# A two-layer hybrid trunk on one core: the second MLP's W2 with activations stationary, and TensorE's MLP loops written out

## The chip, the core and the metric

The kernel runs on one core of a Trainium2 chip. Its time is the device time of one execution in microseconds (us), and lower is better. The engines are TensorE (PE, with its weight loads listed apart as PEld), VectorE (DVE), ScalarE (ACT), GpSimd (POOL) and SyncE (SP), which issues most transfers here.

## The reference, cut to what matters

The input is 256 frames of 2048 values. 16 meta tokens are put ahead of them, which makes 272 tokens; two layers follow, and the meta tokens are dropped at the end. Layer 0 has a state-space mixer, layer 1 windowed attention; behind each mixer stands a dense MLP. Everything is float32.

```python
def squared_relu_mlp(h, w1, w2):          # w1: 2048 x 8192, w2: 8192 x 2048
    a = jax.nn.relu(h @ w1)
    return (a * a) @ w2

for i in range(DEPTH):                    # DEPTH = 2
    hn = rms_norm(h, norm_mix_gain[i])
    ...
    h = h + mix.astype(h.dtype)
    h = h + squared_relu_mlp(rms_norm(h, norm_mlp_gain[i]), mlp_w1[i], mlp_w2[i])
return h[:, N_META:]
```

## The kernel before, in words

**Layout.** The residual `h` stands transposed in SBUF, as 16 tiles of 128 model columns on the partitions by 272 tokens. Every dense product is cut the same way: the weight is the stationary operand, 128 x 128 of it at a time, and the tokens stream past it, 272 in layer 0 and 256 in layer 1's second half, where the meta tokens are no longer needed. The result is again model columns on partitions, so it can be added to `h` as it is.

**Precision.** Each fp32 product is made of three products in the type fp32r: high part by high part, high by low, low by high. ScalarE makes the high part of a weight (`split_hi`, L236, `whi<-raw`), VectorE the low part (`split_lo`, L241, `wlo<-raw,whi`). The activations are split likewise, into `hg_hi` and `hg_lo` for W1 and into `a_hi` and `a_lo` for W2 (the last by `low`, L375).

**Weight stream.** Weights come in halves of 256 rows by 512 columns, 512 KB each, into a ring of RING = 4 slots. SP issues a half (L228) when `lo_split` says that the half four before it has been split; ScalarE may overwrite `whi` when TensorE has used the half four before (`half_used`). The counters run through the whole kernel.

**The MLPs.** An MLP has 8 chunks of 1024 hidden columns. A chunk has six groups: two of W1, each 8 halves for 512 hidden columns, then four of W2, each 4 halves for 512 model columns. `mm_half` multiplies one half: 4 column blocks by 2 row blocks by 3 products, so 24 matmuls, all at L257. That is 384 matmuls for a chunk's W1 and 384 for its W2. Groups take turns in two sets of four PSUM banks. After a W1 group VectorE takes relu and scale out of PSUM (L388), ScalarE squares and rounds (L420, L422), VectorE makes `a_lo` (L375). After a W2 group VectorE adds the four banks to `h` (L397). TensorE may start a group when the group two before it has been taken out (`group_out`), and the third half of a chunk's first W2 group waits for `a_ready` of the second W1 group.

**Loops.** On every engine chunk 0 is written out, chunks 1 to 6 are a hardware loop (`Fori(1, 7)`; TensorE's are L646 in layer 0 and L785 in layer 1), and chunk 7 is written out again. In the loop the counts to wait for are worked out in registers (L250, L267, L361).

**The end.** TensorE transposes the finished `h` back, 32 transposes of 128 x 128 (L794), ScalarE and VectorE copy the banks to `ob` (L1028, L1532), and SP stores eight blocks of 256 KB (L495).

Of the kernel before, what the change touches and what calls it, by code (L numbers as in the profile page):

```python
# [40 lines left out]
RING = 4  # L41
# [47 lines left out]
def trunk(nc, x, meta, g_mix, g_mlp, w_in, log_dt, a_re, a_im, b_re, b_im, c_re, c_im, d_skip,  # L89
# [24 lines left out]
    with ctx:  # L114
# [95 lines left out]
        hg3_lo = at(AR + 34816, "hg3_lo", [128, KT, L], F32R)  # L210
        gained = [(hg_hi, hg_lo)] * 3 + [(hg3_hi, hg3_lo)]

        ob = at(AR + 17408, "ob", [128, 8, 512])
        bias_dram = nc.dram_tensor("bias_by_distance", (NH, NREL), F32, kind="Internal").ap()

        s_raw = [sem(f"raw_landed{k}") for k in range(RING)]
# [122 lines left out]

        def mlp_pe(pe, H, G, layer, c, i, cols):
            def c_val(base, per):
                return base + per * c if i is None else base + per * i
            h0, g0 = (H + 32 * c, G + 6 * c) if i is None else (H, G)
            atok = slice(0, cols.stop - cols.start)
            k = 1 + 2 * layer
            for g in range(2):
                def ready(j):
                    if i is None and c == 0 and g == 0 and j % 2 == 0:  # L350
                        pe.wait_ge(sem("hg_ready"), 4 * k + j // 2 + 1)
                    if i is None and c == 0 and g == 0 and j == 6:
                        pe.wait_ge(sem("group_out"), g0)
                        norm_pe(pe, k, STAT_BANK[k], cols)
                if i is None and c == 0 and g == 1:
                    pe.wait_ge(sem("var_ready"), k + 1)
                mm_group(pe, h0 + 8 * g, i, g0 + g, i, *gained[k], 8, cols, ready)
            for g in range(4):
                def ready(j):
                    if g == 0 and j % 2 == 0:  # L360
                        pe.wait_ge(sem("a_ready"), c_val(16 * layer + j // 2 + 1, 2))  # L361
                mm_group(pe, h0 + 16 + 4 * g, i, g0 + 2 + g, i, a_hi, a_lo, 4, atok, ready)

        def mlp_dve(dve, H, G, layer, c, i, cols, last_chunk):
            h0, g0 = (H + 32 * c, G + 6 * c) if i is None else (H, G)
            n = cols.stop - cols.start
            k = 1 + 2 * layer

            def a_count(m):
                return 16 * layer + 2 * c + m if i is None else 16 * layer + m + 2 * i  # L370

            def low(g):

                dve.wait_ge(sem("a_hi_ready"), a_count(g + 1))
                nc.vector.tensor_tensor(a_lo[:, 4 * g:4 * g + 4, 0:n], asq[:, :, 0:n],  # L375
                                        a_hi[:, 4 * g:4 * g + 4, 0:n], ALU.subtract).then_inc(sem("a_ready"), 1)

            for j in range(32):
                ends = {7: 0, 15: 1, 19: 2, 23: 3, 27: 4, 31: 5}.get(j)
                if ends is not None:  # L380
                    if ends == 0 and i is None and c == 0:
                        norm_rstd_dve(dve, k, cols)
                    dve.wait_ge(sem("half_used"), half(h0 + j + 1, i))
                    src = acc[:, 4 * ((g0 + ends) % 2):4 * ((g0 + ends) % 2) + 4, 0:n]
                    if ends < 2:
                        if layer or ends or i is not None or c:
                            dve.wait_ge(sem("a_sq_ready"), a_count(ends))
                        nc.vector.scalar_tensor_tensor(  # L388
                            out=rbuf[:, :, 0:n], in0=src, scalar=0.0,
                            in1=view(rstd[:, cols], [[0, 4], [1, n]]),  # L390
                            op0=ALU.max, op1=ALU.mult).then_inc(sem("group_out"), 1)
                    else:
                        g = ends - 2

                        dve.wait_ge(sem("group_out"), g0 + ends - 5 if i is None else g0 + ends - 5 + 6 * i)
                        dst = h[:, 4 * g:4 * g + 4, cols]
                        nc.vector.tensor_tensor(dst, dst, src, ALU.add).then_inc(sem("group_out"), 1)  # L397
                if h0 + j + RING < H_END:
                    split_lo(dve, h0 + j + RING, i)
                if ends in (0, 1):  # L400
                    low(ends)
                if last_chunk and ends is not None and ends >= 2 and layer == 0:
                    norm_dve(dve, 2, ends - 2, ALLT)
# [51 lines left out]
        @block.sync  # L455
        def _(sp):
            for tb in range(2):
                sp.dma_start(xs[:, tb, :], x[0, 128 * tb:128 * tb + 128, :]).then_inc(sem("x_landed"), 16)
            sp.dma_start(ms[:, :], meta).then_inc(sem("x_landed"), 16)


            sp.wait_ge(sem("vec_landed"), 16 * 10)

            def stream(h0, w, n_groups, halves, col0=0):
                for g in range(n_groups):
                    for j in range(halves):
                        src = w[256 * j:256 * j + 256, col0 + 512 * g:col0 + 512 * g + 512]
                        load_half(sp, h0 + halves * g + j, None, src.rearrange("(t p) n -> p t n", p=128))

            def stream_mlp(H, layer):  # L470
                with sp.Fori(0, 8) as c:
                    for g in range(2):
                        for j in range(8):
                            src = w1[layer, 256 * j:256 * j + 256, bass.ds(c * 1024 + 512 * g, 512)]
                            load_half(sp, H + 8 * g + j, c, src.rearrange("(t p) n -> p t n", p=128))
                    for g in range(4):
                        for j in range(4):
                            src = w2[layer, bass.ds(c * 1024 + 256 * j, 256), 512 * g:512 * g + 512]
                            load_half(sp, H + 16 + 4 * g + j, c, src.rearrange("(t p) n -> p t n", p=128))

            stream(H_IN, w_in[0], 2, 8)
            stream(H_GLU, w_glu[0], 2, 4)
            stream(H_OUT, w_out[0], 4, 4)
            stream_mlp(H_MLP0, 0)
            stream(H_QKV, w_qkv[0], 1, 8, D)
            stream(H_QKV + 8, w_qkv[0], 4, 8)
            for k, (g, j) in enumerate(WO_ORDER):
                src = w_o[0, 256 * j:256 * j + 256, 512 * g:512 * g + 512]
                load_half(sp, H_WO + k, None, src.rearrange("(t p) n -> p t n", p=128))
            stream_mlp(H_MLP1, 1)  # L490
            for g in range(4):
                for tb in range(2):

                    sp.wait_ge(sem("ob_act" if tb == 0 else "ob_dve"), g + 1)
                    sp.dma_start(out[0, 128 * tb:128 * tb + 128, 512 * g:512 * g + 512],  # L495
                                 ob[:, 2 * g + tb, :]).then_inc(sem("out_landed"), 16)
            sp.wait_ge(sem("out_landed"), 8 * 16)

        @block.tensor
        def _(pe):  # L500
# [141 lines left out]
                mm_group(pe, H_OUT + 4 * g, None, G_OUT + g, None, a_hi, a_lo, 4, ALLT, ready)  # L642


            mlp_pe(pe, H_MLP0, G_MLP0, 0, 0, None, ALLT)
            with pe.Fori(1, 7) as c:  # L646
                mlp_pe(pe, H_MLP0, G_MLP0, 0, None, c, ALLT)
            mlp_pe(pe, H_MLP0, G_MLP0, 0, 7, None, ALLT)


            def kv_stats():
# [129 lines left out]
                    attend(3, k)  # L781


            mlp_pe(pe, H_MLP1, G_MLP1, 1, 0, None, REAL)
            with pe.Fori(1, 7) as c:  # L785
                mlp_pe(pe, H_MLP1, G_MLP1, 1, None, c, REAL)
            mlp_pe(pe, H_MLP1, G_MLP1, 1, 7, None, REAL)

            for g in range(4):
                if g % 2 == 0:  # L790
                    pe.wait_ge(sem("group_out"), G_MLP1 + 47 + g // 2)
                for tb in range(2):
                    for t in range(4):
                        m = tr(acc[:, (2 * g + tb + 4) % 8, 128 * t:128 * t + 128],  # L794
                               h[:, 4 * g + t, NMETA + 128 * tb:NMETA + 128 * tb + 128], ident)
                    m.then_inc(sem("out_tr"), 1)

        @block.scalar
        def _(act):
# [223 lines left out]
            with act.Fori(1, 7) as c:  # L1023
                mlp_act(act, H_MLP1, G_MLP1, 1, None, c, REAL, False)
            mlp_act(act, H_MLP1, G_MLP1, 1, 7, None, REAL, True)
            for g in range(4):
                act.wait_ge(sem("out_tr"), 2 * g + 1)
                nc.scalar.activation(ob[:, 2 * g, :], acc[:, (2 * g + 4) % 8, :], ACT.Copy).then_inc(sem("ob_act"), 1)  # L1028

        @block.gpsimd  # L1030
        def _(pool):
# [81 lines left out]
        def _(dve):  # L1113
# [413 lines left out]
            with dve.Fori(1, 7) as c:  # L1527
                mlp_dve(dve, H_MLP1, G_MLP1, 1, None, c, REAL, False)
            mlp_dve(dve, H_MLP1, G_MLP1, 1, 7, None, REAL, True)
            for g in range(4):  # L1530
                dve.wait_ge(sem("out_tr"), 2 * g + 2)
                v.tensor_copy(ob[:, 2 * g + 1, :], acc[:, (2 * g + 5) % 8, :]).then_inc(sem("ob_dve"), 1)  # L1532


_INS = ["x", "meta_tokens", "norm_mix_gain", "norm_mlp_gain", "s5_w_in", "s5_log_dt", "s5_a_re", "s5_a_im",
# [19 lines left out]
```

## Time and profile before

| | before |
|---|---|
| three runs, median (lowest to highest) | 2160.84 us (2160.17 to 2161.29) |
| profiled execution, span from the first to the last instruction | 2160.0 us |
| mean granted TensorE clock | 0.971 |
| TensorE busy | 2019.7 us (94%), 16332 matmuls |
| VectorE, ScalarE busy | 1244.9 us (58%), 885.8 us (41%) |
| moved by DMA | 338.66 MB, mean 157 GB/s |
| layer 0's MLP, first to last matmul | 318.2 to 1138.2 us |
| layer 1's MLP, first to last matmul | 1423.1 to 2150.7 us |

The profiled execution has no time listed apart from its span; the span is 0.84 us below the median of the three runs. A line of the profile has the form "line engine operation output<-input (partitions x elements, type) xcount | busy us, mean ns of one | idle before it, and what ended most of it". L257 is line 257 of the kernel. A matmul's own duration includes filling and draining, and neighbours overlap; what one matmul costs in a stream is therefore the stretch divided by their number.

### The profile page before, as it was taken

The numbers are of one execution on the slowest core, as the hardware profiler recorded it, in microseconds if no ns is written. First come the engines' busy times: TensorE is split into PE (matmuls) and PEld (weight loads), VectorE is DVE, ScalarE is ACT, GpSimd is POOL, SyncE is SP. The second block draws the span as 40 slices with busy tenths as digits, with TensorE's granted clock in tenths as the row PEclk, the third lists the DMA queues.
The fourth block names the chain that finished last, engine by engine and source line by source line (L and its number), as shares of the span: only waits on it lengthen the run. The fifth ranks groups of instructions, "written<-read, shape, count | busy, mean of one in ns | idle before, by whom it ended". The sixth has DMA issues, their size and how long they took to land.

```text
span 2160.0 us, 39380 instructions
## 1 busy us (share of the span) xinstructions
PE 2019.7 (94%) x16332; PEld 1987.4 (92%) x16332; DVE 1244.9 (58%) x1268; ACT 885.8 (41%) x1047; POOL 155.9 (7%) x91
## 2 busy tenths in 40 slices
PE   6575797999999999999999999999999999999998
PEld 5475797999999999999999888999999999999998
DVE  6989773544545454545476666665555555555554
ACT  4251353343424343434355445554434444344443
POOL 2837300000000000000000011000000000000000
PEclk9797898999999999999999999999999999999999
DMA  6211157555555555555554423556565655656564
GB/s 183 61 43 30 57 177 169 175 174 159 176 152 175 153 175 157 176 153 175 176 170 148 142 89 113 171 167 198 187 187 185 181 189 185 186 185 184 185 185 137
DMA packets 188846, 338.66 MB, mean 157 GB/s; under 512 B 23112, under 2 KB 27416, under 8 KB 188376
## 3 DMA queue, kind: packets, MB, share of 16 engines
q1 hardware_dynamic: 171200, 331.52, 49.4%
q10 hardware_dynamic: 17384, 4.77, 1.4%
q8 instruction: 113, 1.85, 0.3%
q0 software_dynamic: 128, 0.34, 0.1%
q14 instruction: 21, 0.17, 0.0%
HBM read 334.11 MB, written 2.14 MB: 156 GB/s over the span
## 4 chain that ended last, share of the span: by engine, by line
PE 85%; DVE 11%; issue 2%; ACT 1%; ACTq 1%; DMA 0%; SPq 0%; DVEq 0%
PE acc L257 80%; DVE wlo L241 2%; DVE z L1311 1%; ACTq L927 1%; PE acc L717 1%; DVE tb L1328 1%; PE acc L721 1%; DVE hg_lo L289 1%; PE acc L690 0%; DMA ms<-in_meta_tokens 0%; DVE rot L1302 0%; DVE z L1305 0%; PE acc L588 0%; DVE rot L1308 0%; PE acc L704 0%
## 5 line engine op out<-in xcount | busy, mean ns | idle before, releaser
L241 DVE TENSOR_TENSOR wlo<-raw,whi 128x1024 fp32r<-128x1024 f32 x624 | 767.8, 1235 | 712.9 <-ACT whi L236 712.7
L236 ACT ACTIVATE whi<-raw 128x1024 fp32r<-128x1024 f32 x624 | 658.8, 1058 | 1086.4 <-PE acc L257 1066.7
L257 PE MATMUL acc<-hg_hi,whi 128*128 128x256 f32 (+1 forms) x2496 | 722.7, 290 | 54.4 <-DVE wlo L241 38.7
L257 PE MATMUL acc<-hg_hi,wlo 128*128 128x256 f32 (+1 forms) x2496 | 718.7, 288 | 11.1 <-issue 11.1
L257 PE MATMUL acc<-hg_lo,whi 128*128 128x256 f32 (+1 forms) x2496 | 716.2, 287 | 0.0
L257 PE MATMUL acc<-a_hi,whi 128*128 128x272 f32 (+1 forms) x2176 | 619.0, 284 | 1.5 <-DVE a_lo L1374 1.5
L257 PE MATMUL acc<-a_hi,wlo 128*128 128x272 f32 (+1 forms) x2176 | 617.9, 284 | 0.0
L257 PE MATMUL acc<-a_lo,whi 128*128 128x272 f32 (+1 forms) x2176 | 616.4, 283 | 0.0
L257 PEld LDWEIGHTS acc<-hg_hi,whi 128*128 128x128 f32 x2496 | 479.3, 192 | 72.4 <-issue 42.4
L257 PEld LDWEIGHTS acc<-hg_lo,whi 128*128 128x128 f32 x2496 | 477.4, 191 | 0.1
L257 PEld LDWEIGHTS acc<-hg_hi,wlo 128*128 128x128 f32 x2496 | 477.3, 191 | 0.0
L257 PEld LDWEIGHTS acc<-a_hi,whi 128*128 128x128 f32 x2176 | 409.3, 188 | 1.7 <-DVE a_lo L1374 1.7
L257 PEld LDWEIGHTS acc<-a_lo,whi 128*128 128x128 f32 x2176 | 409.5, 188 | 0.0
L257 PEld LDWEIGHTS acc<-a_hi,wlo 128*128 128x128 f32 x2176 | 408.6, 188 | 0.0
L397 DVE TENSOR_TENSOR h<-h,acc 128x1088 f32<-128x1088 f32 (+1 forms) x64 | 80.3, 1254 | 50.4 <-PE acc L257 50.4
L588 PE MATMUL acc<-um,wb 128*128 128x136 f32 x256 | 43.9, 343 | 34.5 <-DVE z L1305 32.6
L588 PEld LDWEIGHTS acc<-um,wb 128*128 128x128 f32 x256 | 42.5, 247 | 36.1 <-ACT um L863 28.9
L257 PE MATMUL acc<-o_hi,whi 128*128 128x256 f32 x256 | 72.5, 283 | 0.0
L257 PE MATMUL acc<-o_lo,whi 128*128 128x256 f32 x256 | 71.8, 280 | 0.0
L257 PE MATMUL acc<-o_hi,wlo 128*128 128x256 f32 x256 | 71.8, 280 | 0.0
L1099 POOL DMA_DIRECT2D kk<-kk x4 | 2.2, 562 | 930.4 <-DVE kk L1504 930.4
L375 DVE TENSOR_TENSOR a_lo<-asq,a_hi 128x1088 fp32r<-128x1088 f32 (+1 forms) x32 | 40.3, 1259 | 37.5 <-ACT a_hi L422 37.5
(235 smaller groups left out, 1283.9 us busy)
## 6 DMA issues: line engine op xcount, KB each, us to landing
raw<-in_mlp_w SPq DMA_DIRECT2D x512, 512.0 KB, 3.8
raw<-in_attn_w_qkv SPq DMA_DIRECT2D x40, 512.0 KB, 3.7
raw<-in_attn_w_o SPq DMA_DIRECT2D x32, 512.0 KB, 4.0
raw<-in_s_w_in SPq DMA_DIRECT2D x16, 512.0 KB, 4.1
raw<-in_s_w_out SPq DMA_DIRECT2D x16, 512.0 KB, 4.8
raw<-in_s_w_glu SPq DMA_DIRECT2D x8, 512.0 KB, 3.8
xs<-in_x SPq DMA_DIRECT2D x2, 1024.0 KB, 7.5
bias_w<-bias_by_distance ACTq DMA_DIRECT2D x2, 1024.0 KB, 13.7
```

Of the source, the lines that this page charges most:

```text
L236: nc.scalar.activation(whi[:, k, :, :], raw[:, k, :, :], ACT.Copy).then_inc(sem("hi_split"), 1)
L241: nc.vector.tensor_tensor(wlo[:, k, :, :], raw[:, k, :, :], whi[:, k, :, :], ALU.subtract).then_inc(sem("lo_split"), 1)
L257: m = nc.tensor.matmul(o, w[:, k, t, 128 * n:128 * n + 128], xx[:, kt + t, cols], start=first and t == 0 and j == 0 and not (packed and n ...
L289: last = nc.vector.scalar_tensor_tensor(out=gained[k][1][:, t, cols], in0=h[:, t, cols], scalar=vecs[:, V_GAIN + 16 * k + t:V_GAIN + 16 * ...
L375: nc.vector.tensor_tensor(a_lo[:, 4 * g:4 * g + 4, 0:n], asq[:, :, 0:n], a_hi[:, 4 * g:4 * g + 4, 0:n], ALU.subtract).then_inc(sem("a_read ...
L397: nc.vector.tensor_tensor(dst, dst, src, ALU.add).then_inc(sem("group_out"), 1)
L588: m = nc.tensor.matmul(acc[:, a, CHUNKS * part:CHUNKS * (part + 1)], wb[:, i, 1 - r, part, :], um[i % 2][:, a, r::2], start=part == 0 and ...
L717: nc.tensor.matmul(o, vw[:, 2 * pr + cp, n, :], ptw[:, par::2, CHUNK * cp:CHUNK * cp + CHUNK], start=cp == 0, stop=False, skip_group_check ...
L721: m = nc.tensor.matmul(acc[rows, 7, 128 * t:128 * t + 128], vm[:, n, 2 * t + par, :], ptm[:, :], start=False, stop=True, skip_group_check= ...
L927: act.dma_start(bias_m[64 * par:64 * par + 64, pr, :, :], bass.AP(bd.tensor, first, [[1, 64], [NREL, NH], [1, NMETA]])).then_inc(sem("bias ...
L1311: op = v.tensor_tensor_scan(out=zz[:, a, part, :], data0=view(prm[:, MAGT, 4 * i + a:4 * i + a + 1], [[0, CHUNKS]]), data1=rot[:, a, part, ...
L1328: stt(out=tb[:, :], in0=tb[:, :], scalar=1.0, in1=yb[:, i % 2, :], op0=ALU.add, op1=ALU.mult).then_inc(sem("t_made"), 1)
```

## The change

It does three things. TensorE's two MLPs are written out, 8 chunks each, with constants in their waits; the other engines keep their loops. In layer 1's MLP, W2 is multiplied the other way round (`mlp1_pe`): 128 columns of `a_hi` or `a_lo`, which are 128 tokens, are stationary, and a row block of the weight half streams by with all its 512 columns, so that the result has tokens on partitions and fills one bank for each of the two token blocks. The residual of these tokens is put into the banks at chunk 0, by 32 fp32 matmuls of `h` with the identity (8 ahead of each of the four groups); VectorE copies the two banks of chunk 0 to `out_rows`, and adds those of chunks 1 to 7 to it. At the end the transposes, the copies and `ob` are gone, and SP stores four blocks of 512 KB straight from `out_rows`.

```diff
+        out_rows = at(HG, "out_rows", [128, 2, D])
...
+        def mlp1_pe(pe, c):
...
+            for g in range(4):
+                bank = 4 * ((g0 + 2 + g) % 2)
+                pe.wait_ge(sem("group_out"), g0 + 1 + g)
+                if c == 0:
+                    for tb in range(2):
+                        for t in range(4):
+                            nc.tensor.matmul(acc[:, bank + tb, 128 * t:128 * t + 128],
+                                             h[:, 4 * g + t, NMETA + 128 * tb:NMETA + 128 * tb + 128], ident,
+                                             start=t == 0, stop=False, skip_group_check=True)
+                for j in range(4):
+                    if g == 0 and j % 2 == 0:
+                        pe.wait_ge(sem("a_ready"), 16 + 2 * c + j // 2 + 1)
+                    pe.wait_ge(sem("lo_split"), h0 + 16 + 4 * g + j + 1)
+                    k = (h0 + 16 + 4 * g + j) % RING
+                    for t in range(2):
+                        for tb in range(2):
+                            rows = slice(128 * tb, 128 * tb + 128)
+                            for n, (xx, w) in enumerate(((a_hi, whi), (a_lo, whi), (a_hi, wlo))):
+                                m = nc.tensor.matmul(acc[:, bank + tb, :], xx[:, 2 * j + t, rows], w[:, k, t, :],
+                                                     start=c > 0 and j == 0 and t == 0 and n == 0,
+                                                     stop=j == 3 and t == 1 and n == 2, skip_group_check=True)
+                    m.then_inc(sem("half_used"), 1)
...
-                        dst = h[:, 4 * g:4 * g + 4, cols]
-                        nc.vector.tensor_tensor(dst, dst, src, ALU.add).then_inc(sem("group_out"), 1)
+                        if layer:
+                            src = acc[:, 4 * ((g0 + ends) % 2):4 * ((g0 + ends) % 2) + 2, :]
+                            dst = out_rows[:, :, 512 * g:512 * g + 512]
+                        else:
+                            dst = h[:, 4 * g:4 * g + 4, cols]
+                        if layer and i is None and c == 0:
+                            nc.vector.tensor_copy(dst, src).then_inc(sem("group_out"), 1)
+                        else:
+                            nc.vector.tensor_tensor(dst, dst, src, ALU.add).then_inc(sem("group_out"), 1)
...
+                sp.wait_ge(sem("group_out"), G_MLP1 + 44 + g + 1)
+                sp.dma_start(out[0].rearrange("(b p) n -> p b n", p=128)[:, :, 512 * g:512 * g + 512],
+                             out_rows[:, :, 512 * g:512 * g + 512]).then_inc(sem("out_landed"), 16)
...
-            mlp_pe(pe, H_MLP0, G_MLP0, 0, 0, None, ALLT)
-            with pe.Fori(1, 7) as c:
-                mlp_pe(pe, H_MLP0, G_MLP0, 0, None, c, ALLT)
-            mlp_pe(pe, H_MLP0, G_MLP0, 0, 7, None, ALLT)
+            for c in range(8):
+                mlp_pe(pe, H_MLP0, G_MLP0, 0, c, ALLT)
...
-            mlp_pe(pe, H_MLP1, G_MLP1, 1, 0, None, REAL)
-            with pe.Fori(1, 7) as c:
-                mlp_pe(pe, H_MLP1, G_MLP1, 1, None, c, REAL)
-            mlp_pe(pe, H_MLP1, G_MLP1, 1, 7, None, REAL)
+            for c in range(8):
+                mlp1_pe(pe, c)
```

The order of TensorE's instructions shows it at two places. The first is the end of a chunk of layer 0's MLP. Before, where the loop turns (ISA and REGISTER_ALU rows set the counts to wait for):

```order
L257 MATMUL acc<-a_hi,whi 128x272
L257 MATMUL acc<-a_lo,whi 128x272
L257 MATMUL acc<-a_hi,wlo 128x272
L646 REGISTER_ALU
L646 COMPARE_AND_BRANCH
L257 MATMUL acc<-hg_hi,whi 128x272 [waits lo_split,group_out]
L257 MATMUL acc<-hg_lo,whi 128x272
```

The same place in the changed kernel, between chunks 1 and 2:

```order
L257 MATMUL acc<-a_hi,whi 128x272
L257 MATMUL acc<-a_lo,whi 128x272
L257 MATMUL acc<-a_hi,wlo 128x272
L257 MATMUL acc<-hg_hi,whi 128x272 [waits lo_split,group_out]
L257 MATMUL acc<-hg_lo,whi 128x272
```

The branch and the register work are gone, and the matmuls of the next chunk are the next instructions in memory.

The second place is the start of W2 in chunk 0 of layer 1's MLP, in the changed kernel (L382 is the residual, `cst` the identity; L394 the product, of which a half now has 12):

```order
L257 MATMUL acc<-hg_hi,wlo 128x256
L382 MATMUL acc<-cst,h 128x128 [waits group_out]
L382 MATMUL acc<-cst,h 128x128 x7
L394 MATMUL acc<-whi,a_hi 128x512 [waits lo_split,a_ready]
L394 MATMUL acc<-whi,a_lo 128x512
L394 MATMUL acc<-wlo,a_hi 128x512
L394 MATMUL acc<-whi,a_hi 128x512
```

And the end of the program before:

```order
L257 MATMUL acc<-a_lo,whi 128x256
L257 MATMUL acc<-a_hi,wlo 128x256
L794 MATMUL acc<-cst,h 128x128 [waits group_out]
L794 MATMUL acc<-cst,h 128x128 x15
L794 MATMUL acc<-cst,h 128x128 [waits group_out]
L794 MATMUL acc<-cst,h 128x128 x15
```

In the changed kernel the last W2 matmul is the last instruction of TensorE's work: the turning of the residual has moved from the end to chunk 0.

## Rows read from the trace of the kernel before

**Rows 1.** The page: TensorE's row, and the chain that ended last.
```profile
PE 2019.7 (94%) x16332; PEld 1987.4 (92%) x16332; DVE 1244.9 (58%) x1268; ACT 885.8 (41%) x1047; POOL 155.9 (7%) x91
...
PE 85%; DVE 11%; issue 2%; ACT 1%; ACTq 1%; DMA 0%; SPq 0%; DVEq 0%
```

**Rows 2.** Windows, layer 0's MLP: stretch, us, PE busy, PEclk, DMA share, GB/s.
```profile
430.40:526.60 96.20, 96.20 (x770) 1.00 0.57 176
...
526.60:629.00 102.40, 98.13 (x770) 0.98 0.53 165
629.00:735.60 106.60, 99.31 (x770) 0.97 0.53 163
735.60:838.60 103.00, 98.74 (x769) 0.97 0.54 164
838.60:941.40 102.80, 98.89 (x769) 0.97 0.53 164
941.40:1042.00 100.60, 97.76 (x769) 0.98 0.54 164
1042.00:1138.10 96.10, 96.10 (x769) 1.00 0.56 173
```

**Rows 3.** Timeline of PE where the loop turns: start us, us, instruction [idle before].
```profile
526.51 0.28 PE L257 MATMUL acc<-a_hi,wlo 128*128 128x272 f32 x1
529.27 0.39 PE L257 MATMUL acc<-hg_hi,whi 128*128 128x272 f32 x1 [2.49 <-issue]
...
531.94 0.38 PE L257 MATMUL acc<-hg_hi,wlo 128*128 128x272 f32 x1 [1.78 <-issue]
```

**Rows 4.** Source lines L646 and L785: duration ns min/median/max, first and last start.
```profile
L646 PEldq COMPARE_BRANCH  x6: 79/4283/4519, 524.5 to 1039.8; - x6
...
L785 PEldq COMPARE_BRANCH  x6: 76/208/237, 1604.4 to 2057.9; - x6
```

**Rows 5.** DMA by queue, 430.4 to 1042 us, then 1606 to 2060 us.
```profile
q8 instruction: 51, 0.84, 0.5%
...
q1 hardware_dynamic: 43599, 84.04, 60.1%
issues: line engine op xcount, KB each, median us to landing
raw<-in_mlp_w SPq DMA_DIRECT2D x161, 512.0 KB, 3.9
```

**Rows 6.** Windows, layer 1's MLP: W2 of chunk 0, W1 and W2 of chunk 1.
```profile
1470.60:1515.69 45.09, 45.09 (x386) 1.00 0.60 188
1515.69:1561.28 45.59, 45.59 (x387) 1.00 0.59 185
1561.28:1606.39 45.11, 45.11 (x387) 1.00 0.61 188
```

**Rows 7.** Windows, `a_lo` in the eight W2 stretches of layer 1: their sum.
```profile
sum 360.90, PE 285.23 PEld 192.66 DVE 9.81; mean PE 35.65 PEld 24.08 DVE 1.23
```

**Rows 8.** Timeline, plain fp32 matmuls: L304 (4 as 8 records), L573 (32 as 64).
```profile
1440.23 1.89 PE L304 MATMUL acc<-ssq,cst 128*128 128x256 f32 x8
...
136.65 7.23 PEld L573 LDWEIGHTS acc<-cc,bp 128*128 128x128 f32 x64
```

**Rows 9.** Timeline of DVE in chunk 1 of layer 1.
```profile
1564.93 1.23 DVE L375 TENSOR_TENSOR a_lo<-asq,a_hi 128x1024 fp32r<-128x1024 f32 x1 [1.09 <-ACT a_hi L422]
```

**Rows 10.** The page: groups of L241, L236 and L397, and the weights' DMA.
```profile
L241 DVE TENSOR_TENSOR wlo<-raw,whi 128x1024 fp32r<-128x1024 f32 x624 | 767.8, 1235 | 712.9 <-ACT whi L236 712.7
L236 ACT ACTIVATE whi<-raw 128x1024 fp32r<-128x1024 f32 x624 | 658.8, 1058 | 1086.4 <-PE acc L257 1066.7
...
L397 DVE TENSOR_TENSOR h<-h,acc 128x1088 f32<-128x1088 f32 (+1 forms) x64 | 80.3, 1254 | 50.4 <-PE acc L257 50.4
...
raw<-in_mlp_w SPq DMA_DIRECT2D x512, 512.0 KB, 3.8
```

**Rows 11.** Timeline of the end, all engines, and L495's time to landing.
```profile
2150.43 0.28 PE L257 MATMUL acc<-a_hi,wlo 128*128 128x256 f32 x1
2150.45 3.51 PEld L794 LDWEIGHTS acc<-cst,h 128*128 128x128 f32 x32
...
2150.75 1.22 DVE L397 TENSOR_TENSOR h<-h,acc 128x1024 f32<-128x1024 f32 x1 [8.90 <-PE acc L257]
...
2151.81 4.62 SPq L495 DMA_DIRECT2D out<-ob  x8
...
2154.24 0.69 DVE L1532 COPY ob<-acc 128x512 f32<-128x512 f32 x1 [0.18 <-PE acc L794]
...
DMA to landing us min/median/max: 2.5/3.5/3.8
```

More of the change, by code:

```diff
@@ L211, in trunk @@
         gained = [(hg_hi, hg_lo)] * 3 + [(hg3_hi, hg3_lo)]
-        ob = at(AR + 17408, "ob", [128, 8, 512])
+        out_rows = at(HG, "out_rows", [128, 2, D])
         bias_dram = nc.dram_tensor("bias_by_distance", (NH, NREL), F32, kind="Internal").ap()
@@ L338, in trunk, with mlp_pe @@
         STAT_BANK = [7, 4 * ((G_MLP0 + 1) % 2), 4 * ((G_QKV + 1) % 2), 4 * ((G_MLP1 + 1) % 2)]
[L342 to L345, printed above, removed]
+        def mlp_pe(pe, H, G, layer, c, cols):
+            h0, g0 = H + 32 * c, G + 6 * c
             atok = slice(0, cols.stop - cols.start)
@@ L349, in ready @@
                 def ready(j):
-                    if i is None and c == 0 and g == 0 and j % 2 == 0:
+                    if c == 0 and g == 0 and j % 2 == 0:
                         pe.wait_ge(sem("hg_ready"), 4 * k + j // 2 + 1)
-                    if i is None and c == 0 and g == 0 and j == 6:
+                    if c == 0 and g == 0 and j == 6:
                         pe.wait_ge(sem("group_out"), g0)
                         norm_pe(pe, k, STAT_BANK[k], cols)
-                if i is None and c == 0 and g == 1:
+                if c == 0 and g == 1:
                     pe.wait_ge(sem("var_ready"), k + 1)
-                mm_group(pe, h0 + 8 * g, i, g0 + g, i, *gained[k], 8, cols, ready)
+                mm_group(pe, h0 + 8 * g, None, g0 + g, None, *gained[k], 8, cols, ready)
             for g in range(4):
@@ L360, in ready @@
                     if g == 0 and j % 2 == 0:
-                        pe.wait_ge(sem("a_ready"), c_val(16 * layer + j // 2 + 1, 2))
-                mm_group(pe, h0 + 16 + 4 * g, i, g0 + 2 + g, i, a_hi, a_lo, 4, atok, ready)
+                        pe.wait_ge(sem("a_ready"), 16 * layer + 2 * c + j // 2 + 1)
+                mm_group(pe, h0 + 16 + 4 * g, None, g0 + 2 + g, None, a_hi, a_lo, 4, atok, ready)
+        def mlp1_pe(pe, c):
+            h0, g0 = H_MLP1 + 32 * c, G_MLP1 + 6 * c
+            for g in range(2):
+                def ready(j):
+                    if c == 0 and g == 0 and j % 2 == 0:
+                        pe.wait_ge(sem("hg_ready"), 12 + j // 2 + 1)
+                    if c == 0 and g == 0 and j == 6:
+                        pe.wait_ge(sem("group_out"), g0)
+                        norm_pe(pe, 3, STAT_BANK[3], REAL)
+                if c == 0 and g == 1:
+                    pe.wait_ge(sem("var_ready"), 4)
+                mm_group(pe, h0 + 8 * g, None, g0 + g, None, *gained[3], 8, REAL, ready)
+            for g in range(4):
[20 more added lines that the diff above has]
+                    m.then_inc(sem("half_used"), 1)
@@ L491, in _ @@
             for g in range(4):
[L492 to L497, printed above, removed]
+                sp.wait_ge(sem("group_out"), G_MLP1 + 44 + g + 1)
+                sp.dma_start(out[0].rearrange("(b p) n -> p b n", p=128)[:, :, 512 * g:512 * g + 512],
+                             out_rows[:, :, 512 * g:512 * g + 512]).then_inc(sem("out_landed"), 16)
+            sp.wait_ge(sem("out_landed"), 4 * 16)
         @block.tensor
@@ L781, in _ @@
                     attend(3, k)
-            mlp_pe(pe, H_MLP1, G_MLP1, 1, 0, None, REAL)
-            with pe.Fori(1, 7) as c:
-                mlp_pe(pe, H_MLP1, G_MLP1, 1, None, c, REAL)
-            mlp_pe(pe, H_MLP1, G_MLP1, 1, 7, None, REAL)
[L789 to L796, printed above, removed]
+            for c in range(8):
+                mlp1_pe(pe, c)
         @block.scalar
@@ L1025, in _ @@
             mlp_act(act, H_MLP1, G_MLP1, 1, 7, None, REAL, True)
-            for g in range(4):
-                act.wait_ge(sem("out_tr"), 2 * g + 1)
-                nc.scalar.activation(ob[:, 2 * g, :], acc[:, (2 * g + 4) % 8, :], ACT.Copy).then_inc(sem("ob_act"), 1)
         @block.gpsimd
@@ L1529, in _ @@
             mlp_dve(dve, H_MLP1, G_MLP1, 1, 7, None, REAL, True)
-            for g in range(4):
-                dve.wait_ge(sem("out_tr"), 2 * g + 2)
-                v.tensor_copy(ob[:, 2 * g + 1, :], acc[:, (2 * g + 5) % 8, :]).then_inc(sem("ob_dve"), 1)
 _INS = ["x", "meta_tokens", "norm_mix_gain", "norm_mlp_gain", "s5_w_in", "s5_log_dt", "s5_a_re", "s5_a_im",
```

## The prediction

> **What bounds the kernel now.** I read the page first: TensorE is busy for 94% of the span and holds 85% of the chain that ended last [rows 1]. So what counts is how long TensorE's stream of matmuls is, and where it has holes. The view by windows gives both. In layer 0's MLP a whole chunk (768 matmuls of 272 columns) takes 96.2 us where it runs undisturbed, in chunk 1 and in chunk 7, which is 125.3 ns a matmul at a granted clock of 1.00; chunks 2 to 6 take 102.4, 106.6, 103.0, 102.8 and 100.6 us, at 0.97 or 0.98 [rows 2]. The timeline shows the holes: where the loop turns, nothing starts for 2.5 us, five matmuls run, then again nothing for 1.8 us, and both idle times end by "issue", so TensorE waited for no other engine [rows 3]. The branch that turns the loop takes 4.3 us in the median [rows 4], and the queue that brings TensorE's instructions is active all the while: 51 packets of 16 KB in 612 us, so one each 12 us [rows 5].
>
> Layer 1's MLP has the same loop and no such holes. There the branch takes 0.2 us [rows 4], the instruction queue is absent from 1606 to 2060 us [rows 5], and chunk 1's W1 and W2 take 45.59 and 45.11 us with TensorE busy throughout [rows 6]. The loop's body evidently stays at hand in layer 1, while in layer 0 it is fetched anew each turn.
>
> **Part 1, layer 0's MLP written out.** With the branch gone, chunks 2 to 6 should run like chunks 1 and 7. Chunk 7 is the right model: it is straight-line code today, fetched as it goes, and has no hole. From 526.6 to 1042.0 us are 515.4 us; 5 x 96.2 = 481.0. **Gain 34.4 us**, holes and the slower clock behind them together. The weights must keep up without those pauses: chunk 7 did at 173 GB/s and layer 1 runs at 185 to 188 [rows 2, 6], so they will. The low end, if a third of the excess is something else, is 23 us.
>
> The Trainium skill (Runtime: NRT & Kernel Launch, section Instruction fetch mechanics) says that TensorE holds 128 KiB of instructions, refilled in blocks of 16 KiB, and that a taken branch to a target outside what is held stalls for a fetch. Layer 0's turns agree; layer 1's five do not, at 0.2 us each. By the rule alone layer 1's loop would have lost another 34 us, and writing it out would bring the time to about 2079; the trace leaves nothing there to gain.
>
> **Part 2, layer 1's MLP written out.** Zero, for the reason just given: no hole to close.
>
> **Part 3, W2 of layer 1 turned round.** Today its eight W2 stretches add up to 360.9 us [rows 7] for 8 x 384 = 3072 matmuls of 256 columns: 117.5 ns each. The change makes 1536 of 512 columns, so the columns streamed are the same, and only what a matmul costs beyond its columns can be saved. At 2.4 GHz, which the granted clock of 1.00 is, 256 columns are 106.7 ns; 10.8 ns are left over. No row has fp32r at 512 columns, so the price is bounded:
> - Above: the remainder grows with the columns. 256 columns cost 118.1 ns over a whole chunk (45.59 + 45.11 = 90.70 us by 768) [rows 6] and 272 cost 125.3 [rows 2]: both 0.461 ns a column. Then twice 117.5 = 235 ns, and the gain is zero.
> - Below: the remainder vanishes behind a longer stream. Plain fp32 records pass at two clocks a column: of 256 columns they are (1.89 - 0.38) / 7 = 0.216 us apart (0.38 is one record's own length), of 128 columns 7.23 / 64 = 0.113 us [rows 8]. So a record with 512 clocks of stream costs 216 ns, and one with 256 costs more than half of that. At 216 ns W2 takes 331.8 us, a gain of 29.1.
> - Taken: the remainder stays as it is per matmul, 117.5 + 106.7 = 224.2 ns. It lies between the two, and the 272 and 256 column rows allow it too (7.2 ns for 16 columns, where the clock alone gives 6.7). 1536 x 224.2 = 344.4 us. **Gain 16.5 us.**
>
> What lies beside it: VectorE's step after a group has the same 1024 elements per partition, from two full banks where it had four half-full ones (1.25 us, [rows 10]), and stays hidden under the next group. The supply must go faster: a half lasts 12 x 224 = 2.69 us where it lasted 2.82, which asks for 195 GB/s where 188 flowed at 0.60 of the DMA engines' time [rows 6]. From issue to ready a half takes 3.8 + 1.06 + 1.24 = 6.1 us [rows 10], and four slots give it 10.8. No wait. The wait nearest to biting is `a_ready` at the third half: `a_lo` is ready at 1564.93 + 1.23 = 1566.16, 4.88 us after W2's start at 1561.28 [rows 6, 9]. TensorE gets there after two halves, 5.6 us before and 5.38 after. 0.5 us of slack are left, 0.3 even at 216 ns. I book zero, and 8 x 0.2 us at worst.
>
> **Part 4, the residual in chunk 0.** 32 plain fp32 matmuls of 128 columns. L573 has just this form: 32 of them appear as 64 records in 7.23 us [rows 8]. They stand in TensorE's stream with nothing to hide them. **Loss 7.2 us.** Chunk 0's copy on VectorE in place of the add is of the same size and hidden.
>
> **Part 5, the end.** Today the last matmul ends at 2150.71 and the span at 2160.0: 9.3 us, of which 3.5 are the 32 transposes, and behind the last copy at 2154.93 come 5.1 us for SP's last two issues and the landing [rows 11]. Afterwards: 1.26 us for VectorE's last add, then one store. SP issues today one by one, the last at about 2155.8, so 0.85 of the 5.1 us were a queue that is gone; a store of 512 KB in place of 256 KB may give back 0.5. So 1.26 + 4.7 = 6.0 us. **Gain 3.3 us.** The first three stores go out during the last chunk, behind the last weights on SP's queue, which nothing waits for. A gain of 2 to 4 is possible.
>
> **Sum.** -34.4 - 16.5 + 7.2 - 3.3 = -47.0 us. The profiled span of 2160.0 becomes 2113.0; the median of the runs stands 0.84 above the span, so 2160.84 - 47.0 = **2113.8 us**.
>
> The Trainium skill (TensorE: Matmul & The Clock Gate, section Back-to-back issue gap) puts matmuls that follow each other at full clock N / 2.4 + 2.5 ns apart. At 256 columns that is 109 ns against the 117.5 measured here, so the trace does not bear it out for this pattern. At 512 it would be 216, the low bound above, and the sum would then be 2101.
>
> **Rivals.**
> - *Hidden remainder.* At twice the stream the weight load disappears: 216 ns, 2113.8 - 12.6 = 2101.2 us. For it: the fp32 records. Against it: those records draw half as many values per clock.
> - *Proportional remainder.* 512 columns cost 235 ns: 2113.8 + 16.5 = 2130.3 us, and turning W2 round alone loses 3.9 us (the residual less the end). For it: 0.461 ns a column in both widths.
> - *The stall is not the loop's.* If the long code of layer 0 meets the same holes, the 34.4 us stay: 2148.2 us. Chunk 7 speaks against it. This is also the case in which the first part of the change doesn't do what it says.
> - *Slower.* The weights as moving operand stream while ScalarE and VectorE write the neighbouring slots of the same ring; today they are only read in 128-column loads. If that slows the stream, the change loses from the point where a 512-column matmul costs more than 224.2 + 47.0 / 1.536 = 254.8 ns. At 265 ns it would be 2113.8 + 62.7 = 2176.5 us. W1 and W2 today differ by only 1 ns though their operands lie in different places, which gives this little weight.
>
> **How the numbers follow.** The remainder per matmul 0.46 (2113.8), hidden 0.22 (2101.2), proportional 0.23 (2130.3), loop's holes stay 0.04 (2148.2), slower 0.03 (2176.5), and 0.02 for holes that stay together with a proportional remainder (2148.2 + 16.5 = 2164.7), which is within 0.2%, 4.3 us, about what a measurement of this kernel can tell from no change. The range goes from 2099, which is the hidden case with a gain of 36 in layer 0, to 2132, the proportional case with the small losses at `a_ready`; it leaves out about 1 in 10. Faster by over 0.2%: 0.95; within: 0.02; slower: 0.03.
>
> **What would show it.** Windows over layer 0's MLP should give 96.2 us for every chunk, without idle time that "issue" ends, and the clock near 1.00. The rows of L394 over a W2 stretch, divided by 192, give the price: 224 is the forecast, 216 and 235 the rivals. L382 should show 64 records in 7.2 us. `group_out` to span end should be near 6 us, and no PE row should wait for `a_lo`. A PE idle time on `wlo` in W2, or chunks of layer 0 still over 100 us, would prove the working wrong.

## The result, and the profile after

The changed kernel takes **2124.53 us** in the median (2122.09 to 2127.72, 4 runs), the kernel before, run beside it, 2160.51 us (2159.52 to 2161.29). The ratio is 0.9832, with a 95% interval from 0.982 to 0.9844: 36.0 us faster. Forecast were 2113.8 us, with a range from 2099 to 2132. The profiled execution took 2125.94 us, with a span of 2124.1 us.

The page of the changed kernel, the rows that answer to [rows 1]:

```profile
span 2124.1 us, 35935 instructions
...
PE 2010.8 (95%) x14828; PEld 1912.2 (90%) x14828; DVE 1240.7 (58%) x1264; ACT 883.5 (42%) x1043; POOL 160.5 (8%) x91
...
PE 86%; DVE 10%; issue 1%; ACT 1%; ACTq 1%; DMA 1%; SPq 0%; DVEq 0%
PE acc L257 65%; PE acc L394 17%; DVE wlo L241 2%; DVE z L1335 1%; ACTq L954 1%; DVE tb L1352 1%; PE acc L728 1%; PE acc L755 1%; PE acc L759 1%; DVE hg_lo L289 1%; DMA ms<-in_meta_tokens 1%; DVE rot L1326 0%; DVE z L1329 0%; PE acc L628 0%
```

TensorE still holds the chain, and the new line L394 is 17% of the span.

Windows of the changed kernel over layer 0's MLP, chunks 1 to 7 (columns as in [rows 2], which they answer to):

```profile
430.50:526.70 96.20, 96.20 (x770) 1.00 0.56 176
526.70:622.90 96.20, 96.20 (x771) 1.00 0.56 175
622.90:719.10 96.20, 96.20 (x770) 1.00 0.57 175
719.10:815.30 96.20, 96.20 (x770) 1.00 0.57 175
815.30:911.50 96.20, 96.20 (x770) 1.00 0.58 175
911.50:1007.70 96.20, 96.20 (x770) 1.00 0.58 175
1007.70:1103.90 96.20, 96.20 (x770) 1.00 0.56 172
```

Every chunk takes 96.20 us at a granted clock of 1.00, and TensorE is never idle. Chunks 2 to 6 took 515.4 us and take 481.0: 34.4 us less, as booked.

The eight W2 stretches of layer 1's MLP in the changed kernel, by windows (first, second and last, and the sum of all eight; they answer to [rows 6, 7]):

```profile
1437.19:1488.81 51.62, 51.62 (x258) 1.00 0.51 165
1534.41:1578.91 44.50, 44.50 (x194) 1.00 0.58 191
...
2075.01:2119.51 44.50, 44.50 (x194) 1.00 0.48 155
sum 363.12, PE 363.12; mean PE 45.39
```

They were 360.9 us and are 363.1: with the residual in them they have grown. 44.50 us for 192 matmuls are **231.8 ns** for 512 columns (forecast 224.2). The first stretch carries the residual, and is 51.62 - 44.50 = 7.1 us longer than the others (booked 7.2):

```profile
1437.20 1.95 PE L382 MATMUL acc<-cst,h 128*128 128x128 f32 x16
1438.90 0.48 PE L394 MATMUL acc<-whi,a_hi 128*128 128x512 f32 x1
1439.22 0.39 PE L394 MATMUL acc<-whi,a_lo 128*128 128x512 f32 x1
```

That is TensorE's timeline at the first of the four groups. 16 records take 1438.90 - 1437.20 = 1.70 us, and the first matmul behind them takes 0.32 us to the next one where 0.23 are usual: 1.8 us a group. Eight stretches of 44.50 us would be 356.0 us, 4.9 less than before (booked 16.5).

The end, in the timeline of the changed kernel, answers to [rows 11]:

```profile
2119.28 0.40 PE L394 MATMUL acc<-wlo,a_hi 128*128 128x512 f32 x1
2119.71 1.22 DVE L439 TENSOR_TENSOR out_rows<-out_rows,acc 128x1024 f32<-128x1024 f32 x1 [8.74 <-PE acc L394]
2120.96 0.37 SPq L535 DMA_DIRECT2D out<-out_rows  x1
```

From the last matmul's end at 2119.68 to the end of the span are 4.4 us, where it was 9.3: 4.9 gained (booked 3.3).

So: -34.4 (layer 0) - 4.9 (W2) + 7.1 (residual) - 4.9 (end) = -37.1 us. The spans differ by 35.9; of the other 1.2 us, 0.8 lie between the two MLPs (1138.1 to 1470.6 us before, 1103.9 to 1437.2 after), where nothing was changed.

### The profile page after: what moved, and what is told of

Its sections match the earlier page's. It is cut to its first block, busy times and chain, and to the rows that moved or that the text cites. A ratio compares the mean times of both kernels' runs of the same rounds, so it can differ in the third digit from the quotient of the medians.

```text
span 2124.1 us, 35935 instructions
## 1 busy us (share of the span) xinstructions
PE 2010.8 (95%) x14828; PEld 1912.2 (90%) x14828; DVE 1240.7 (58%) x1264; ACT 883.5 (42%) x1043; POOL 160.5 (8%) x91
## 4 chain that ended last, share of the span: by engine, by line
PE 86%; DVE 10%; issue 1%; ACT 1%; ACTq 1%; DMA 1%; SPq 0%; DVEq 0%
PE acc L257 65%; PE acc L394 17%; DVE wlo L241 2%; DVE z L1335 1%; ACTq L954 1%; DVE tb L1352 1%; PE acc L728 1%; PE acc L755 1%; PE acc L759 1%; DVE hg_lo L289 1%; DMA ms<-in_meta_tokens 1%; DVE rot L1326 0%; DVE z L1329 0%; PE acc L628 0%; DVE rot L1332 0%
## 5 line engine op out<-in xcount | busy, mean ns | idle before, releaser
L241 DVE TENSOR_TENSOR wlo<-raw,whi 128x1024 fp32r<-128x1024 f32 x624 | 769.8, 1239 | 684.5 <-ACT whi L236 684.3
L236 ACT ACTIVATE whi<-raw 128x1024 fp32r<-128x1024 f32 x624 | 658.7, 1058 | 1057.8 <-PE acc L257 830.2
L257 PE MATMUL acc<-a_hi,whi 128*128 128x272 f32 x1152 | 331.2, 287 | 1.5 <-DVE a_lo L1398 1.5
L257 PE MATMUL acc<-a_hi,wlo 128*128 128x272 f32 x1152 | 332.5, 289 | 0.0
L257 PE MATMUL acc<-a_lo,whi 128*128 128x272 f32 x1152 | 330.8, 287 | 0.0
L257 PEld LDWEIGHTS acc<-a_hi,whi 128*128 128x128 f32 x1152 | 217.0, 188 | 1.7 <-DVE a_lo L1398 1.7
L257 PEld LDWEIGHTS acc<-a_lo,whi 128*128 128x128 f32 x1152 | 216.7, 188 | 0.0
L257 PEld LDWEIGHTS acc<-a_hi,wlo 128*128 128x128 f32 x1152 | 216.3, 188 | 0.0
L394 PE MATMUL acc<-wlo,a_hi 128*128 128x512 f32 x512 | 202.2, 395 | 0.0
L394 PE MATMUL acc<-whi,a_hi 128*128 128x512 f32 x512 | 202.1, 395 | 0.0
L394 PE MATMUL acc<-whi,a_lo 128*128 128x512 f32 x512 | 201.2, 393 | 0.0
L394 PEld LDWEIGHTS acc<-wlo,a_hi 128*128 128x128 f32 x512 | 96.2, 188 | 22.5
L394 PEld LDWEIGHTS acc<-whi,a_lo 128*128 128x128 f32 x512 | 96.3, 188 | 22.1
L394 PEld LDWEIGHTS acc<-whi,a_hi 128*128 128x128 f32 x512 | 96.5, 188 | 21.5
```

Of the source, the lines that this page charges most:

```text
L236: nc.scalar.activation(whi[:, k, :, :], raw[:, k, :, :], ACT.Copy).then_inc(sem("hi_split"), 1)
L241: nc.vector.tensor_tensor(wlo[:, k, :, :], raw[:, k, :, :], whi[:, k, :, :], ALU.subtract).then_inc(sem("lo_split"), 1)
L257: m = nc.tensor.matmul(o, w[:, k, t, 128 * n:128 * n + 128], xx[:, kt + t, cols], start=first and t == 0 and j == 0 and not (packed and n ...
L394: m = nc.tensor.matmul(acc[:, bank + tb, :], xx[:, 2 * j + t, rows], w[:, k, t, :], start=c > 0 and j == 0 and t == 0 and n == 0, stop=j = ...
```

## The experiments

Two questions were open. Is the gain all in layer 0's loop, and why does that loop stall where layer 1's, of the same size, does not? And why do 512 columns cost 231.8 ns?

### The two halves of the change, each alone

**Written out, W2 as it was (unroll01).**

```diff
             mlp_pe(pe, H_MLP0, G_MLP0, 0, 0, None, ALLT)
-            with pe.Fori(1, 7) as c:
-                mlp_pe(pe, H_MLP0, G_MLP0, 0, None, c, ALLT)
-            mlp_pe(pe, H_MLP0, G_MLP0, 0, 7, None, ALLT)
+            for c in range(1, 8):
+                mlp_pe(pe, H_MLP0, G_MLP0, 0, c, None, ALLT)
```

and the same in layer 1. Expected:

> The kernel before with TensorE's MLPs written out in both layers and W2 of layer 1 left as it was. If the gain of the change is all in layer 0's loop and the turned W2 is worth nothing by itself: chunks 2 to 6 of layer 0 take 96.2 us each, layer 1's chunks 90.7 us as before, and the time is 2160.5 - 34.4 = about 2126 us, within 3 us of the change's 2124.5. If the turned W2 carries part of the gain (the forecast's 16.5 us), this kernel stays clearly above the change, near 2137.

Measured: 2128.52 us against 2162.23, ratio 0.9846 (0.9831 to 0.9861), 33.7 us faster. The first case holds, though the time is 4.0 us above the change's and not within 3; the kernel before stood 1.7 us higher beside it. 2137 is ruled out. VectorE's loop, which keeps step, turns from 527.5 to 1008.6 us in layer 0, 96.2 us a chunk, and from 1573.8 to 2027.2 us in layer 1, 90.7 us a chunk as before.

**Turned round, layer 0's loop put back (turned_loop0).** The last lines of the change's diff, for layer 0, undone. Expected:

> The change with layer 0's MLP put back into its loop; layer 1 turned round and written out. By the trace of the change: W2 saves (117.5 x 2 - 231.8) x 1536 = 4.9 us, the residual's 64 records cost about 7, the end gives 4.9: together 2 to 3 us below the kernel before, about 2158. By the forecast's sum it would be 12.6 us below, 2148. Layer 0's chunks 2 to 6 must show 101 to 107 us again.

Measured: 2158.43 us against 2162.23, ratio 0.9984 (0.9975 to 0.9993), 3.8 us faster: the 12.6 us that the forecast's sum would give are ruled out. The branch that turns layer 0's loop takes 4.3 us again (min/median/max in ns, first and last start in us):

```profile
L688 PEldq COMPARE_BRANCH  x6: 79/4286/4528, 521.9 to 1038.7; - x6
```

From the first turn to the last are 516.8 us, so 103.4 for each of the chunks 2 to 6. The two halves add up, 33.7 + 3.8 = 37.5 against 36.0 for the change, within what the runs scatter.

### Why layer 0's loop stalls

An obvious rival is a wait for VectorE. TensorE's idle times in the kernel before, from 430 to 1042 us (total, times, longest):

```profile
PE acc L257 <- issue: 16.1, 7, 2.9
PE acc L257 <- DVE h L397: 6.5, 3, 2.3
```

Three of them are put down to VectorE's add of the group just finished. But the program waits there for the group two before, and the changed kernel has the same add and the same wait and no idle time in these chunks. So VectorE is not what the 22.6 us wait for, and they go with the loop. The other 11.8 of the 34.4 us are longer busy time, 492.8 us for chunks 2 to 6 in place of 481.0, at a mean granted clock of 0.97.

A packet of the instruction queue is 16 KB (0.84 MB in 51 of them [rows 5]). In the changed kernel's straight code 39 of them come from 430 to 1042 us, one each 15.7 us, in which TensorE runs 125 matmuls and 125 weight loads: some 256 instructions a packet, which I call a block. Counted in the built program before, layer 0's loop runs from instruction 5053 to 6630, layer 1's from 14315 to 15892; in blocks from 19.74 to 25.90 and from 55.92 to 62.08. Both are 6.2 blocks long, and touch 7 or 8 blocks by where the blocks' ends lie. TensorE's records in the trace agree: 1578 a turn, and 5010 and 14270 up to the two loops (layer 0's five further turns taken off the second), 43 and 45 fewer than counted.

**The loop moved by a few instructions (pad24, pad48, pad8).** Only this is added ahead of layer 0's MLP, with 48, 96 and 16 waits for a count that was reached long before; two waits make one instruction.

```diff
+            for _ in range(96):
+                pe.wait_ge(sem("cst_landed"), 16 - _ % 2)
             mlp_pe(pe, H_MLP0, G_MLP0, 0, 0, None, ALLT)
```

Expected of the first two, which ran together, and of the third, made after them:

> The kernel before with 24 instructions more on TensorE ahead of layer 0's MLP (48 waits for a count that is long reached), so that both loops lie 24 instructions later in memory. Theory: the loop's 1577 instructions take 7 or 8 blocks of 256 (one packet of the instruction queue is 16 KB), by where they start; layer 0's start about 30 instructions short of a block's end and so take 8, which don't stay at hand, layer 1's take 7. 24 instructions don't carry layer 0's loop over the block's end: chunks 2 to 6 take 101 to 107 us as before, the branch 4 us. Rival, the extra waits or any change of the code cure it: 96.2 us.

> The same with 48 instructions more. Theory of the blocks: layer 0's loop now starts in the next block and takes 7, so chunks 2 to 6 take 96.2 us each, the branch 0.2 us, the instruction queue is silent in both loops, and the time is about 2127 us, as with the loops written out (unroll01, 2128.5). Rival, layer 0's loop stalls for another reason (its 272 columns, its waits, its place beside other engines' loops): 2161 us as before.

> The kernel before with 8 instructions more ahead of layer 0's MLP (16 waits). pad24 had cured layer 0, where the theory of the blocks with its end put 30 instructions away had expected none, so either the block's end is nearer (between 8 and 24 instructions from the loop's start, as the time of the packet just behind it allows) or extra waits cure it wherever the loop lies. Block's end between 8 and 24: chunks 2 to 6 still take 101 to 107 us, about 2161 in all. Waits as such, or a block's end within 8: 96.2 us and about 2128.

Measured: pad8 2165.7 us (one run), pad24 2129.51 us (one run), pad48 2128.48 us against 2160.2 (ratio 0.9854, 0.9838 to 0.9869). The branch that turns layer 0's loop, in pad24, pad8 and pad48 in turn (ns, min/median/max):

```profile
L648 PEldq COMPARE_BRANCH  x6: 76/210/243, 525.6 to 1006.6; - x6
```

```profile
L648 PEldq COMPARE_BRANCH  x6: 79/4196/4403, 525.2 to 1043.8; - x6
```

```profile
L648 PEldq COMPARE_BRANCH  x6: 76/208/236, 525.0 to 1006.0; - x6
```

8 instructions leave the 4.2 us branch, 24 make it 0.2 us. My guess of 30 instructions to the block's end, for which pad24 should still have stalled, was wrong; the end lies between 8 and 24. From the first turn to the last pad8 takes 518.6 us, 103.7 a chunk. What it is that matters, the place or the waits, pad8 alone does not say; the next run, put on record together with pad24 and pad48, bears on that.

**Layer 1's loop moved off its good place (swap).** The 96 waits of pad48, and 352 more ahead of layer 1's MLP. Expected:

> 48 instructions more ahead of layer 0's MLP and 176 more ahead of layer 1's. Theory of the blocks: layer 0 is cured as in pad48, and layer 1's loop now starts 0.93 block later and takes 8 blocks: its chunks 2 to 6 take about 97 us in place of 90.7, with TensorE's branch at 4 us and packets on the instruction queue between 1606 and 2060 us; the total is within 10 us of the kernel before (the 352 waits ahead of layer 1 may cost some us once). Rival: layer 1's loop has no holes wherever it lies.

Windows of swap: layer 0's chunk 2; layer 1's chunks 1, 2 and 3.

```profile
524.80:621.00 96.20, 96.20 (x770) 1.00 0.57 174
...
1501.70:1592.40 90.70, 90.70 (x770) 1.00 0.62 187
1592.40:1691.50 99.10, 93.39 (x770) 0.97 0.56 171
1691.50:1790.70 99.20, 92.80 (x770) 0.97 0.56 171
```

Its branch in layer 1, its timeline where that loop first turns, and its DMA from 1592 to 2085 us:

```profile
L789 PEldq COMPARE_BRANCH  x6: 79/4546/4993, 1590.4 to 2085.5; - x6
```

```profile
1592.33 0.28 PE L257 MATMUL acc<-a_hi,wlo 128*128 128x256 f32 x1
1598.32 0.58 PE L257 MATMUL acc<-hg_hi,whi 128*128 128x256 f32 x1 [5.71 <-issue]
```

```profile
q8 instruction: 45, 0.74, 0.6%
```

The holes have changed places: layer 0's loop is clean, and layer 1's, which never stalled, now loses 8.3 us a turn, with 45 packets fetched, nine a turn, where the kernel before had none [rows 5]. Layer 0's loop in the kernel before fetched as many: of the 51 packets of [rows 5] six belong to chunk 1, and from 526.6 to 1042 us there are 45. The waits as such do not cure a loop, since here they stand right ahead of the one that stalls. The nine places (in blocks: 19.74, 19.77 and 56.79 stall; 19.83, 19.93, 55.92, 55.95, 56.01 and 56.11 do not) fit one rule: with a block's end at about 0.80 to 0.83 of my count, the stalling loops touch 8 blocks and the others 7. The place of the block's end is fitted to these runs, and my first guess of it was wrong; what was on record ahead of its run is that 48 instructions cure layer 0 and that layer 1 then stalls in swap. Layer 1's loop was made to stall at this one place only. The total is 2189.39 us (one run), 29 above the kernel before and not within 10 of it: the 352 waits cost 20 us themselves (layer 1's loop starts at 1499.8 us here and at 1479.9 in pad48; the 96 ahead of layer 0 do not show, since its loop starts at 428.7 us here and at 428.3 before), and a turn costs 8.3 us, not the 6.3 I had put down.

The Trainium skill (Runtime: NRT & Kernel Launch, Instruction fetch mechanics) gives TensorE room for 8 blocks of 256 instructions. The sizes agree with these runs, 16 KB a packet and some 256 instructions; that a loop which touches 8 blocks is fetched anew each turn is what they add. Why the eighth makes the difference was not tried.

### What 512 columns cost

**Matmuls alone behind the kernel's work (bench_end).** Eight stretches like this one, when ScalarE, VectorE and the weights' transfers have finished:

```diff
+            pe.wait_ge(sem("group_out"), G_MLP1 + 48)
+            for r in range(48):
+                mm(acc[:, r % 2, :], a_hi[:, r % 8, 0:128], whi[:, r % 4, r % 2, :], start=True, stop=True)
```

> The change with eight stretches of matmuls put behind the last W2 group, when ScalarE, VectorE and the weights' transfers are idle: fp32r with 512, 384, 256 and 128 columns streaming past 128 stationary ones, the old form (weights stationary, 256 activations streaming), 512 columns past 32 stationary ones, plain fp32 with 512, and bf16 with 512. Their results are not used. Theory 1, the fp32r stream itself is slower than a column per clock: the first stretch costs 232 ns a matmul as in the kernel, and 384, 256 and 128 columns follow 4.3 + 0.4445 per column, 175, 118 and (if the weight load does not bind) 61. Theory 2, the other engines' traffic slows it: 216 to 219 ns at 512. Theory 3, the weight load beside it slows it: with 32 stationary columns the 512 cost clearly less than with 128. Plain fp32 should take 427 to 432 ns (two records of 216), bf16 216.

TensorE's timeline there (start us, us, line, shape; a row is 48 records). The stretch less the last record's own length, by 47, is the price:

```profile
2119.97 11.40 PE L829 MATMUL acc<-whi,a_hi 128*128 128x512 f32 x48 [1.31 <-DVE out_rows L439]
2131.21 8.52 PE L831 MATMUL acc<-whi,a_hi 128*128 128x384 f32 x48
2139.56 5.83 PE L833 MATMUL acc<-whi,a_hi 128*128 128x256 f32 x48
2145.23 5.47 PE L835 MATMUL acc<-whi,a_hi 128*128 128x128 f32 x48
2150.54 5.88 PE L837 MATMUL acc<-a_hi,whi 128*128 128x256 f32 x48
2156.26 11.28 PE L839 MATMUL acc<-whi,a_hi 128*32 128x512 f32 x48
2167.38 20.76 PE L841 MATMUL acc<-raw,h 128*128 128x512 f32 x48
2187.98 10.52 PE L843 MATMUL acc<-whi,a_hi 128*128 128x512 bf16 x48
```

With a record's length of 0.40, 0.34, 0.28 us and so on: fp32r with 512 columns 234 ns (232 in the median; the first one took 344), 384 columns 174, 256 columns 118 with activations stationary and 119 with weights stationary, 128 columns about 111, 512 columns past 32 stationary ones 232, bf16 216. Each plain fp32 record of 512 columns takes 429 ns; my expectation counted it as two of 216, a slip, since a call is two records.

Theory 2 falls: with ScalarE and VectorE idle and a granted clock of 1.00, 512 columns cost what they cost in the kernel. Theory 3 falls: a weight load of 32 columns, 108 ns in place of 188, changes nothing. What is left is the first: an fp32r column takes (232 - 118) / 256 = 0.445 ns, where bf16 of the same shape takes 216 / 512 = 0.42 all told, and only some 4 ns a matmul don't depend on the columns. The line 4.3 + 0.4445 per column gives 118, 125.2, 175 and 231.9 ns for 256, 272, 384 and 512; measured are 118, 125.3, 174 and 231.8. At 128 columns the line does not hold: they cost 111 ns, not 61. What holds them up was not tried. Why fp32r is slower by 6% a column stays open.

### A version that is faster than both

**The residual by transposes (tr_residual, tr_again).**

```diff
                             nc.tensor.matmul(acc[:, bank + tb, 128 * t:128 * t + 128],
                                              h[:, 4 * g + t, NMETA + 128 * tb:NMETA + 128 * tb + 128], ident,
-                                             start=t == 0, stop=False, skip_group_check=True)
+                                             start=t == 0, stop=False, is_transpose=True, skip_group_check=True)
```

> The change with the 32 residual matmuls made as transposes (one record of about 109 ns each in place of two of 112), still laid into the banks that W2 then adds to. If a transpose leaves the bank in a state to which the next matmuls add: 3.3 us less than the change, with 32 records in 3.5 us. If the records cost the same, no difference.

Measured: 2119.94 us against 2162.23, ratio 0.9811 (0.9796 to 0.9825). Since the intervals of this and the change overlap, both ran again on one chip:

> The change itself once more, beside tr_again on the same chip. 2122 to 2128 us, as before.

> tr_residual once more, beside the change on the same chip: 3.3 us less than it (32 records of 109 ns in place of 64 of 112); the means should differ by 2 to 5 us.

The change 2123.55 us (2122.14 to 2125.99), with transposes 2119.72 (2116.73 to 2121.86), no run of one within the other's: 3.8 us faster. Its source row has half the records:

```profile
L382 PE MATMUL acc<-cst,h x32: 270/273/273, 1431.6 to 1468.4; 128*128 128x128 f32 x32
```

**Loop kept, but well placed (pad_tr).** Layer 0 as in pad48, layer 1 as in tr_residual.

> Layer 0's MLP in its loop behind 48 more instructions, layer 1's turned round and written out, the residual by transposes. If placing the loop is worth as much as writing it out, this is within 3 us of tr_residual's 2119.9 us, and so 4 to 5 us below the change; otherwise 34 us above.

Measured: 2121.30 us (2120.59 to 2121.96) against 2160.2, ratio 0.9819 (0.9806 to 0.9833). 48 instructions ahead of a loop are worth as much as writing out 8 chunks, within 1.4 us. The best of all runs is the change with transposes, 2119.7 to 2119.9 us.

## Why the prediction was right

**Part 1** (34.4 us) was right to the tenth in the windows, and its reason, that the loop is fetched anew each turn, was right. What it left open, why layer 1's is not, is a matter of place: between 8 and 24 instructions decide it for layer 0. The single chunks of [rows 2] were not all cut at the same place of a turn, and 106.6 us holds part of the next hole: from branch to branch chunks 2 to 6 take 102.2, 104.1, 103.2, 102.9 and 102.9 us. Their sum stays. **Part 2** (zero) was right for this kernel: in unroll01 layer 1's chunks take 90.7 us as before. By the rule of the Trainium skill (Runtime: NRT & Kernel Launch, Instruction fetch mechanics), as the prediction used it, 34 us more should have gone there; they did not. That section gives both a room of 128 KiB, which holds a loop of 6.2 blocks, and a window of two pages for a branch's target, which does not, and layer 1's turns of 0.2 us bear out the first. swap shows that layer 1 could have stalled too, had its loop lain otherwise.

**Part 3** is the term that was mis-sized: 16.5 us booked, 4.9 measured. That is 11.6 us, a little more than the 10.7 by which the time missed. The step that failed is the value taken between the bounds, "the remainder stays as it is per matmul". It doesn't: of the 11 ns beyond the clock's columns at 256, 4 are per matmul and 7 grow with the columns. The rows to see it were there, 118.1 ns at 256 and 125.3 at 272, and a line through them is 0.45 ns a column. The prediction read them as allowing a fixed remainder, 7.2 ns for 16 columns against the clock's 6.7; but that half nanosecond in 16 columns is some 8 in 256. The lower bound rested on plain fp32 records, which stream at another pace and did not bear on fp32r. Of the two bounds the upper one, 235 ns, was near. The N / 2.4 + 2.5 of the Trainium skill (TensorE: Matmul & The Clock Gate, Back-to-back issue gap) fits bf16, at 216 ns, and not this type; the same section also gives about 131 ns at 512 columns for a stream with weight loads, which no type here reached. `a_ready` and the supply did not bite, as booked: no PE row waits for `a_lo`.

**Part 4**: 7.2 booked, 7.1 measured. **Part 5**: 3.3 booked, 4.9 measured; the span ends 3.1 us after the last store's issue began, where it ended 4.2 us after before, behind a queue of eight. The sum booked -47.0 and the parts measured -37.1: they are 0, +11.6, -0.1 and -1.6 us apart.

One more thing was slightly off: I set the profiled span 0.84 us below the time of a run. In the runs here the time stands 1.8 us above the span each time.

Of the rivals, the proportional remainder was nearest (2130.3), and the truth lies between it and the forecast, nearer to the rival: it had a chance of 0.23, the forecast's own mechanism 0.46. The time lies in the range because the range was drawn to hold that rival too, not because the remainder was understood. The slower case had nothing in it: weights as the moving operand stream no slower than activations, 118 against 119 ns with nothing beside them, and no slower while ScalarE and VectorE write the neighbouring slots, 231.8 ns in the kernel against 232 in bench_end.

## What to carry to other kernels

When an engine's idle time is ended by "issue" and its instruction queue moves while a loop turns, look at where the loop lies before writing it out: here two loops of 6.2 blocks differed by 5 x 6.9 us only through their place, and a few instructions ahead cured one. A matmul's price per column is to be taken from rows of its own type at two widths. And turning a product round was worth little here, where the columns streamed stay the same: W2 gave 4.9 us and its residual took 7.1. What paid was the end, 4.9 us, where the transposes, the copies and a queue of stores went.

## What the runs showed of the hardware that I had not expected

- By the rule fitted above, a loop of 1577 instructions on TensorE that touches 7 blocks of 256 turns in 0.2 us without a fetch; over 8 blocks it is fetched anew, 45 packets in five turns, and loses 6.9 us a turn in layer 0 and 8.3 in layer 1, the lower clock included.
- fp32r streams at 0.445 ns a column from 256 to 512 columns, at a granted clock of 1.00, with or without other engines at work, and at 512 with 128 or 32 stationary columns alike (232 ns), where bf16 keeps to 0.42.
- 352 waits that are long satisfied cost TensorE 20 us in swap, 56 ns each; two make one instruction, and 174 such records follow each other there from 1387.3 to 1406.0 us. The 96 ahead of layer 0 do not show in the time.
- Matmuls add to a bank that fp32 transposes have filled: in tr_residual these stand in for the matmuls with the identity, with `start` set on the first of each bank alone.
